# Stage orders rewritten in a two-layer hybrid DeltaNet, attention and Mamba-2 step, and six stored slots per DeltaNet tile in place of seven

## The reference

```python
h    = rms_norm(x, norm_w) * (1 + scale) + shift        # shift, scale, gate = silu(cond) @ w_mod + b_mod
proj = h @ w_in                                          # 1024 -> 8800 columns, split over the mixers
a    = gated_rms(gdn(forward) + rev(gdn(backward)))      # DeltaNet, 4 heads of 128, chunks, two directions
b    = softmax_attention(rope(norm(q)), rope(norm(k)), v) * silu(z_b)          # 8 heads, 2 KV heads, 64
c    = rms_norm((ssd(forward) + rev(ssd(backward)) + D * x) * silu(z_c), ssm_norm_w)  # 16 heads of 64
merged = sig(g_a) * (a @ w_branch_a) + sig(g_b) * (b @ w_branch_b) + sig(g_c) * (c @ w_branch_c)
x = x + gate * (merged @ w_out)
```

## Time and profile before

| | before |
|---|---|
| median of 3 runs | 4101.25 us (4098.83 to 4103.64) |
| profiled execution | 4097.26 us, span 4095.5 us |
| PE busy | 3728.9 us, 91% of the span |
| DVE / ACT / POOL busy | 52% / 26% / 19% |
| chain that ended last | PE 60%, issue 10%, DVE 9%, DMA 8% |
| DMA | 521 MB, mean 127 GB/s |

### The profile page before, as it was taken

How to read it: one execution, slowest core, us unless ns; L and a number is a source line. 1 busy time by engine, 2 the same in 40 slices (tenths; PEclk the granted TensorE clock), 3 DMA queues, 4 the chain that set the end, 5 groups by cost and what they waited for, 6 DMA issues and landing times.

```text
span 4095.5 us, 71558 instructions
## 1 busy us (share of the span) xinstructions
PE 3728.9 (91%) x29139; PEld 3486.7 (85%) x29139; DVE 2123.8 (52%) x2421; ACT 1049.0 (26%) x1910; POOL 762.4 (19%) x778
## 2 busy tenths in 40 slices
PE   6999999999799788889989999999987987888898
PEld 3999999999688565889989999999986875578898
DVE  3631353233577676586465125523336876846853
ACT  3211120112345461311122102111224546232210
POOL 1110111132400243131011101112232013511400
PEclk8999999999899899999989999999999998999999
DMA  7332232233611467644233322323335117675532
GB/s 221 105 103 87 78 95 90 72 120 107 257 44 37 148 233 240 231 139 106 93 109 116 100 76 82 93 79 99 118 134 192 38 43 235 230 244 186 118 104 86
DMA packets 375283, 521.13 MB, mean 127 GB/s; under 512 B 83089, under 2 KB 293833, under 8 KB 372017
## 3 DMA queue, kind: packets, MB, share of 16 engines
q1 hardware_dynamic: 327992, 393.58, 29.2%
q0 software_dynamic: 36256, 104.28, 9.4%
q10 hardware_dynamic: 10720, 18.88, 1.4%
HBM read 340.20 MB, written 176.45 MB: 126 GB/s over the span
## 4 chain that ended last, share of the span: by engine, by line
PE 60%; issue 10%; DVE 9%; DMA 8%; DVEq 4%; SPq 4%; ACT 2%; POOL 2%; POOLq 0%; ACTq 0%
PE PSUM L807 10%; PE PSUM L808 10%; PE PSUM L809 10%; PE PSUM L1368 3%; DMA proj_d<-leave 3%; PE PSUM L1521 2%; PE PSUM L1355 2%; PE PSUM L1283 2%; PE PSUM L1285 2%; PE PSUM L1284 2%; PE PSUM L1653 2%; PE PSUM L1654 2%; PE PSUM L1655 2%; PE PSUM L1334 1%; DMA qk_t<-proj_d 1%
## 5 line engine op out<-in xcount | busy, mean ns | idle before, releaser
L807 PE MATMUL PSUM<-h_hi,w_hi 128*128 128x384 f32 x2400 | 806.4, 336 | 8.2 <-DVEq L2495 8.2
L808 PE MATMUL PSUM<-h_lo,w_hi 128*128 128x384 f32 x2400 | 804.3, 335 | 0.0
L809 PE MATMUL PSUM<-h_hi,w_lo 128*128 128x384 f32 x2400 | 804.2, 335 | 0.0
L807 PEld LDWEIGHTS PSUM<-h_hi,w_hi 128*128 128x128 f32 x2400 | 452.6, 189 | 12.7 <-DVEq L2495 8.9
L808 PEld LDWEIGHTS PSUM<-h_lo,w_hi 128*128 128x128 f32 x2400 | 452.6, 189 | 0.0
L809 PEld LDWEIGHTS PSUM<-h_hi,w_lo 128*128 128x128 f32 x2400 | 452.5, 189 | 0.0
L2169 POOL DMA_DIRECT2D proj_d<-leave x140 | 142.5, 1018 | 1450.8 <-DVE leave L2491 567.2
L1283 PE MATMUL PSUM<-h_hi,w_hi 128*128 128x384 f32 x960 | 328.0, 342 | 4.0 <-ACT ssm_rows L1806 4.0
L1284 PE MATMUL PSUM<-h_lo,w_hi 128*128 128x384 f32 x960 | 323.8, 337 | 0.0
L1285 PE MATMUL PSUM<-h_hi,w_lo 128*128 128x384 f32 x960 | 323.6, 337 | 0.0
L2599 DVE TENSOR_REDUCE row_max<-PSUM 128x1 f32<-128x1152 f32 x128 | 173.5, 1355 | 98.3 <-PE PSUM L1335 98.2
(11 more groups left out here) (387 smaller groups left out, 7393.7 us busy)
## 6 DMA issues: line engine op xcount, KB each, us to landing
proj_d<-leave POOLq DMA_DIRECT2D x140, 512.0 KB, 3.9
w_raw<-in_w_in SPq DMA_DIRECT2D x54, 1024.0 KB, 5.1
gdn_tile_d<-g_out SPq DMA_DIRECT2D x18, 1792.0 KB, 7.3
wide_br<-proj_d SPq DMA_DIRECT2D x48, 576.0 KB, 4.4
xs<-ssm_tok_d SPq DMA_DIRECT2D x32, 640.0 KB, 5.6
ssm_tok_d<-x_rest SPq DMA_DIRECT2D x36, 512.0 KB, 3.1
w_in<-in_w_in SPq DMA_DIRECT2D x16, 1024.0 KB, 6.2
w_next<-in_w_mod SPq DMA_DIRECT2D x16, 1024.0 KB, 8.4
```

What stands on the lines that cost most here:

```text
L807: pe.matmul(dst, wh, x_hi[:, k, lo:hi], start=(k == 0), stop=False)
L808: pe.matmul(dst, wh, x_lo[:, k, lo:hi], start=False, stop=False)
L809: last = pe.matmul(dst, wl, x_hi[:, k, lo:hi], start=False, stop=(k == kt - 1))
```

## The change

- Tail: DVE does `rotate` and `low_parts` before `split_tail`. SP issues the first `ain` loads before the stores of `ssm_rows`; PE waits for `ssm_rows` before the first turn of heads, and no longer ahead of the tail.
- Start: the load of `w_mod[3]` waits until six token tiles are turned, and shares a semaphore with a token load, so that one becomes free (`w_high`).
- DeltaNet preparation: 6 slots per tile. DVE multiplies bank 4 by each direction's decay (slots 0 and 5), adds the two decays in place, and multiplies bank 3 by the sum once (slot 2: one direction's triangle below the diagonal, the other's above, their sum on it). The scaled keys lie in slots 1 and 4, the values in 3. `solve_begin` halves the diagonal. The scan's loads take slots 2:4 as one piece, and the low or high triangle is read from the same slot.
- SSM preparation: the loads of tile 0's decay rows are issued in the attention stage; the modulation product runs at tiles 1 to 8 in place of 0 to 7, its copy is one of 128x256 in place of four of 2x256, DVE zeroes that bank once in place of two POOL clears.
- SSM scan: the loads of DeltaNet tile 1 are issued by ACT, right behind those of tile 0, in place of SP after the last step; SP arrives at barrier 5 right behind its last scan load and stores the final states afterwards. The first tile of the scan waits for all of them.
- Branches: new places in `BESIDE` (four `y` jobs beside branch b, five beside a); the weight of the SSM norm is multiplied into `w_branch_c` as this is split, so `weigh_y` is gone; the low part `low_y_b` is made by DVE; the high copies of full-depth weights are made by ACT (`weights_high`, semaphore `w_high`), and DVE's `split_in_place` waits for them; `y_sq` is laid out so that ACT writes with a stride of 8 elements and DVE reads it in sequence; all nine `low_o` come before the last `merge_first`.

```diff
--- before.py
+++ after.py
@@ -82,17 +82,12 @@
-BESIDE = ({1: ("y", 0), 3: ("o", 0), 5: ("o", 1), 7: ("y", 1), 9: ("o", 2), 11: ("o", 3), 13: ("o", 4),
-           15: ("o", 5), 17: ("o", 6), 19: ("o", 7), 21: ("o", 8), 23: ("y", 2)},
-          {1: ("y", 3), 4: ("y", 4), 7: ("y", 5), 10: ("y", 6), 13: ("y", 7), 16: ("y", 8)},
+BESIDE = ({1: ("y", 0), 3: ("o", 0), 5: ("o", 1), 6: ("y", 1), 8: ("o", 2), 10: ("o", 3), 12: ("o", 4),
+           13: ("y", 2), 15: ("o", 5), 17: ("o", 6), 19: ("o", 7), 21: ("o", 8), 22: ("y", 3)},
+          {5: ("y", 4), 8: ("y", 5), 11: ("y", 6), 14: ("y", 7), 17: ("y", 8)},
           {})
...
@@ -315,7 +310,7 @@
-        y_sq = place(a, "y_sq", [P, KT, P])
+        y_sq = place(a, "y_sq", [P, P, KT])
...
@@ -671,45 +666,41 @@
-            return (l * (33 - 2 * p) + count) * 16
+            return (l * (33 - 8 * p) + count) * 16
...
@@ -671,45 +666,41 @@
         def tile_loads(e, t):
             for d in range(2):
                 tt = tile_of(t, d)
-                in_ = scan_in[d][t % 2] if t else beta_in
-                e.dma_start(av_t[d][t % 2][:], gdn_tile_d[tt, :, 3 * d:3 * d + 4:3]).then_inc(in_, 16)
+                in_ = scan_in[d][t % 2] if t > 1 else beta_in
+                e.dma_start(av_t[d][t % 2][:], gdn_tile_d[tt, :, 2:4]).then_inc(in_, 16)
                 e.dma_start(qk_t[d][t % 2][:], proj_d[tt, :, B_GDN:B_GDN + 8]).then_inc(in_, 16)
         def kq_loads(e, t):
             for d in range(2):
-                e.dma_start(kq_t[d][t % 2][:], gdn_tile_d[tile_of(t, d), :, 3 * d + 1:3 * d + 3]).then_inc(kq_in[t % 2], 16)
+                e.dma_start(kq_t[d][t % 2][:], gdn_tile_d[tile_of(t, d), :, 4 * d:4 * d + 2]).then_inc(kq_in[t % 2], 16)
...
@@ -776,12 +767,33 @@
         def split_in_place(dve, l, g):
-            n, p = G_ATT + g, g % 2
+            p, last = g % 2, None
             hi, (raw, lo) = (half_hi[p], half_lo[p]) if g < 8 else (full_hi[p], full_lo[p])
-            dve.wait_ge(w_loaded[p], 16 * split_count(l, n // 2) + 16)
-            dve.tensor_copy(hi[:], raw[:])
-            dve.drain()
-            dve.tensor_tensor(lo[:], raw[:], hi[:].bitcast(F32), ALU.subtract).then_inc(w_ready[p], 1)
+            if g < 8:
+                dve.wait_ge(w_loaded[p], 16 * split_count(l, (G_ATT + g) // 2) + 16)
+                dve.tensor_copy(hi[:], raw[:])
+                dve.drain()
+            else:
+                dve.wait_ge(w_high, l * 8 + g - 7)
+            if 8 <= g < 12:
+                for k in range(KT):
+                    last = dve.scalar_tensor_tensor(lo[:, k], raw[:, k], vec[:, V_SNORM + k:V_SNORM + k + 1], hi[:, k].bitcast(F32), ALU.mult, ALU.subtract)
+            else:
+                last = dve.tensor_tensor(lo[:], raw[:], hi[:].bitcast(F32), ALU.subtract)
+            last.then_inc(w_ready[p], 1)
+        def weights_high(act, l, g):
+            n, p, last = G_ATT + g, g % 2, None
+            hi, raw = full_hi[p], full_lo[p][0]
+            act.wait_ge(w_loaded[p], 16 * split_count(l, n // 2) + 16)
+            if 8 <= g < 12:
+                for k in range(KT):
+                    last = act.activation(hi[:, k], raw[:, k], ACT.Copy, scale=vec[:, V_SNORM + k:V_SNORM + k + 1])
+            else:
+                last = act.activation(hi[:], raw[:], ACT.Copy)
+            last.then_inc(w_high, 1)
...
@@ -893,6 +897,16 @@
                 ain_load(0)
                 ain_load(1)
+                sp.wait_ge(row_made, l * 3 + 3)
+                flat_rows = ssmrow_d.rearrange("t d r n -> (t d r) n")
+                sp.dma_start(flat_rows[0:512].rearrange("(c p) n -> p c n", p=P), ssm_rows[:, 0:4].bitcast(F32)).then_inc(row_out, 16)
+                sp.dma_start(flat_rows[512:576], ssm_rows[0:64, 4].bitcast(F32)).then_inc(row_out, 16)
+                sp.wait_ge(row_out, l * 80 + 80)
+                sp.sem_inc(waits_held, 1)
...
@@ -1002,16 +1016,11 @@
-                    sp.wait_ge(ssm_prod[d], l * 17 + 16)
-                    sp.sem_inc(waits_held, 1)
-                tile_loads(sp, 1)
-                inverse_loads(sp, 1)
-                kq_loads(sp, 1)
+                barrier(sp, l, 5)
...
@@ -1268,8 +1279,6 @@
-                pe.wait_ge(row_made, l * 3 + 3)
-                pe.sem_inc(waits_held, 1)
                 for i in range(N_TAIL):
...
@@ -1457,25 +1466,27 @@
-                    if t < NS:
-                        pe.wait_ge(mod_in[t % 2], l * 64 + (t // 2) * 16 + 32)
+                    if t:
+                        pe.wait_ge(mod_in[(t - 1) % 2], l * 64 + ((t - 1) // 2) * 16 + 32)
                         pe.wait_ge(sp_cb, n + 1)
-                        mod_parts(7, w_next[t % 2], GW)
+                        mod_parts(7, w_next[(t - 1) % 2], GW)
...
@@ -1980,6 +1988,9 @@
                 inverse_loads(act, 0)
+                tile_loads(act, 1)
+                kq_loads(act, 1)
+                inverse_loads(act, 1)
...
@@ -2034,42 +2045,43 @@
-                    act.activation(y_sq[:], y_t[:, t], ACT.Square).then_inc(squared, 1)
+                    act.activation(y_sq[:].rearrange("p t k -> p k t"), y_t[:, t], ACT.Square).then_inc(squared, 1)
...
@@ -2034,42 +2045,43 @@
-                for s, (what, t) in BESIDE[0].items():
-                    if s == 23:
-                        act.wait_ge(acc_ready[1], acc_done(l, G_ATT + 3, 1))
-                        for q in range(3):
-                            o_high(q)
+                for what, t in BESIDE[0].values():
                     if what == "y":
                         square_y(t)
                     elif t + 1 < NT:
                         square_o(t + 1)
-                for t in range(3, NT):
+                act.wait_ge(acc_ready[1], acc_done(l, G_ATT + 3, 1))
+                for t in range(NT):
                     o_high(t)
-                act.wait_ge(lo_made, nth(l, NT - 1, 0, 2) + 1)
-                high = 0
-                for _, t in BESIDE[1].values():
-                    while high < t - 1:
-                        y_high_b(high)
-                        high += 1
-                    square_y(t)
-                for t in range(high, NT):
+                act.wait_ge(lo_made, nth(l, NT - 1, 0, 3) + 1)
+                for t in range(4):
                     y_high_b(t)
+                for s in range(24):
+                    if s == 21:
+                        act.wait_ge(y_summed, l * NT + NT)
+                        act.sem_inc(waits_held, 1)
+                    if s == 21:
+                        weights_high(act, l, 8)
+                    if s in BESIDE[1]:
+                        t = BESIDE[1][s][1]
+                        square_y(t)
+                        y_high_b(t)
                 act.wait_ge(acc_ready[1], acc_done(l, G_GDN + 3, 1))
                 for t in range(NT):
                     y_high_a(t)
+                weights_high(act, l, 9)
...
@@ -2243,6 +2259,11 @@
+                def decay_rows(t, d):
+                    pool.dma_start(s_row[d][32:34].rearrange("s h n -> s (h n)"), ssmrow_d[t, d].rearrange("(s h) n -> s (h n)", s=2)).then_inc(s_in[d], 16)
+                    pool.dma_start(s_col[d][0:32], ssmrow_d[t, d]).then_inc(s_in[d], 16)
+                for d in range(2):
+                    decay_rows(0, d)
...
@@ -2310,21 +2327,8 @@
-                def weigh_y(t):
-                    pool.wait_ge(squared, squared_at(l, "y", t))
-                    pool.tensor_tensor(y_t[:, t], y_t[:, t], over(vec[:, V_SNORM:V_SNORM + 8], P), ALU.mult).then_inc(pool_made, 1)
-                def low_y_b(t):
-                    pool.wait_ge(hi_made, nth(l, t, 1, 3) + 1)
-                    pool.tensor_tensor(y_lo[:, t, 4:KT], y_t[:, t, 4:KT], y_hi_b[:, :, cols(t)].bitcast(F32), ALU.subtract).then_inc(pool_made, 1)
-                o_power(0)
-                for what, t in BESIDE[0].values():
-                    if what == "y":
-                        weigh_y(t)
-                    elif t + 1 < NT:
-                        o_power(t + 1)
-                for step, t in Y_STEPS[3:]:
-                    (weigh_y if step == "w" else low_y_b)(t)
+                for t in range(NT):
+                    o_power(t)
...
@@ -2553,12 +2557,13 @@
-                    if i and TAIL + i + 1 < G_ATT:
-                        split_tail(TAIL + i + 1)
                     if i < NT:
                         rotate(i)
                         dve.drain()
                     low_parts(i)
+                    if i and TAIL + i + 1 < G_ATT:
+                        split_tail(TAIL + i + 1)
...
@@ -2581,15 +2586,16 @@
-                        last = dve.tensor_tensor(by_head(g_out[p][:, 2 + 2 * d]), by_head(bank(1)), over(e_rest[:, d, t, 0:4], GD), ALU.mult)
+                        last = dve.tensor_tensor(by_head(g_out[p][:, 1 + 3 * d]), by_head(bank(1)), over(e_rest[:, d, t, 0:4], GD), ALU.mult)
                     last.then_inc(scaled, 1)
                     dve.wait_ge(gp_e, n + 1)
                     dve.wait_ge(gp_k, n + 1)
```

(26 more changed lines are left out.)

108 lines of the change are left out of this document (51 added, 57 removed).

## The result

The changed kernel takes 4024.02 us (median of 4 runs, 4022.17 to 4033.07), the one before 4100.04 us (4 runs, 4093.22 to 4103.64): ratio 0.9821, 95% interval 0.9801 to 0.9841. A second series gave 4032.99 against 4105.72, ratio 0.9824 (0.9802 to 0.9845). The gain is 73 to 76 us by the medians, where 69.4 was forecast.

What follows compares the result with a forecast made beforehand. PE was taken to set the time in most of the span. Five terms, largely one layer doubled, summed to -69.4 us from 4097.3: 4027.9 in the profiled execution, 4032 as median; 8 in 10 lie in 4000 to 4070.

Steps and rivals of the forecast that it cites:

- Tail, -24.8 forecast: Tail, both layers: 21.4 us of PE's waits go and 3.4 of lower clock returns; bounds -28.3 to -12.
- I take half: Tail: the lower clock after PE's waits costs 6.9 us together, of which 3.4 was counted as regained.
- Rival 4: Tail: POOL, not the casts, ends each chain, so the tail gives only 8 us: 4049; chance 0.06.
- DeltaNet preparation, -1.4 forecast: DeltaNet preparation: same DVE time within 0.1, a smaller store waited for less; between -3 and +1 us.
- SSM preparation, -9 forecast: SSM preparation: PE's waits for `s_col` and `w_next` go but don't add up, POOL's later loads hold; -4.5 us per layer.
- Scan and barrier, -8.2 forecast: SSM scan and barrier 5: SP arrives at once, -5.1 us per layer, less contention; bounds -12 and +4 for two layers.
- the +1 taken: SSM scan: tile 1's loads share full DMA engines, so the steps stretch, +1 us per layer.
- The second rival: SSM scan: moved loads halve SP's stream, steps go from 7.2 to 7.6 us, the 8 us are lost: 4040; chance 0.08.
- Branches, -26 forecast: Branches: less DVE load without POOL beside it shortens branch a, branch b pays +3.5; -13 us per layer, bounds -8 to -36.
- the first unit of c, 15.5 becomes 13.7: Start of branch c: the wait for POOL's last low parts goes, -1.8 us per layer.
- Rival 1: Branch a: DVE bounds it whatever POOL does, so the branches give nothing: 4058; chance 0.09.
- Rival 3: Branches: DVE waits at `w_high`, delaying merges and PE's banks; 6.5 us lost per group gives 4109; chance 0.04.

## Why the prediction was right, term by term

The time, 4032 for 4024 to 4033, and the sum, -69.4 for -73 to -76, were right. Their closeness is in part luck: of the terms, two compensate, the tail with 7 us more than forecast and the branches with 9.5 less.

- **Tail, -24.8 forecast, -32 measured**, by the stages outside its own bound of -28.3 (by the times alone, 27 to 42, the bound would still do). Waits and chain were as forecast: all seven waits for `q_hl` gone, both at the start as well, `w_lo` never late. The step that failed is "I take half" of the clock. All of it came back, because no wait was left in the tail for the clock to fall after: the matmuls of its three lines, 975.4 us in all on the page of before, take 967.5, so the clock was worth 7.9. With the 21.4 us of waits that is 29.3. Another 1.6 is in the turns behind the waits, L1259, of which 72 take 9.0 us in a layer in place of 9.8; what is left, under 2 us, no row assigns. Rival 4 is refuted: all seven waits went, not a third of them.
- **DeltaNet preparation, -1.4 forecast**, -1.0 by the stages (2 x -0.5), and open between 0 and 18 by the times, as said. That the stage keeps its length was right.
- **SSM preparation, -9 forecast, -8.8 by the stages and -10.5 alone.** Right in size and mechanism: the waits did not add up, and it is POOL's loads behind the stored inverse that took over. The run with the rows early shows it: moving just these gives another 5.7 per layer.
- **Scan and barrier, -8.2 forecast, -7.7 by the stages, -5.1 alone.** The barrier's 6.7 became 1.6, as worked out (-5.1). Contention is larger than the +1 taken: the SSM scan as a whole gained only 2.0, so it pays some 3 per layer, of which the longer waits for `c_t` are 2.3 in layer 0; the page of the profile has `xs` landing after 7.3 us in place of 5.6. The DeltaNet scan, counted at nothing, is 1.8 shorter (its waits for `qk_t` went from 8.1 to 5.8 in layer 0), but no run shows that this part did it. Without that 1.8 the term by the stages is -4.0, half of the forecast. The second rival, SP's row held down to half of the stream, would have given the 8 us back: the gain of 4 to 8 in all ways of counting speaks against it, though part of its mechanism, the steps made longer by the shared stream, is there.
- **Branches, -26 forecast, -16.5 by the stages**, the term that was mis-sized: -13 per layer was taken, -8.3 came, and the miss is on both sides of the start of branch c. Branches b and a together were to give -16.2 + 3.5 = -12.7; over all layers they gave 4.2 - 13.8 = -9.6. What branch a becomes was right: 59.9 for 59.3, L2828 (now L2841) at 1.36, no POOL, DVE 49.8 of 59. What it comes from was not: 75.5 was read in one layer, where ten layers have 73.6 on average and at most 75.2. In that one layer the change looks like the forecast (140.6 became 128.6, -12.1).
  The second step that failed is "the first unit of c, 15.5 becomes 13.7". From its first matmul, that unit took 14.5 and 16.1 in the kernel before and takes 17.0 and 17.2 in the changed one, and branch c as a whole went from 103.0 to 104.3 on average. The gain was to come from "POOL's last low parts", but POOL had finished them at 1851.6, and what PE waited for until 1858.0 was DVE's `full_lo`, 1.4 us. After the change PE waits 1.7 there for the last `y_lo`, which DVE makes behind the eight parts of `full_lo` (3.25 us from 1815.87), and then does 5.6 us at the lower of its two levels (0.79 over 16 us). One thing that was covered at nothing lies ahead of it: ACT's write of `y_sq` over a stride takes 2.20 and not 1.06, and the last sum on DVE waited 1.7 for it. But it is not what the wait at branch c hangs on alone, since with the squares in the old order the wait is 2.6: DVE's last two sums then take 1.5 longer, against 1.1 less of waiting for ACT.
- **Rival 1**, POOL innocent of the long additions, is refuted by POOL's work put back: the addition is at 2.03 again, and branch a at 72.5 where it was 73.6 before. The branches as a whole are then above those of before (246 for 241.4), because branch b keeps the jobs that were moved beside it. Rival 3 did not come up: no wait for `w_high` by DVE reached PE.

## What to carry to other kernels

Where two operations run on one engine between a wait's release and the next engine's need, put what is needed first and the large split behind it; here that was worth more than all else, and the clock came back with the waits. An elementwise step on POOL that nobody waits for is still paid for by DVE's copies and additions of two SBUF inputs beside it (39 us of POOL beside branch a cost DVE 15.6 us and made the branch 12.7 longer), so folding it into a weight split can gain time. When two waits in a row are removed, look for the third (here a DMA issue parked behind a store it does not need) before adding them up, and look for the last operation of a stage, since PE can lose more by the clock behind a wait of under 2 us than by the wait. And read a stage's length in both layers, and in more than one profile if there are any, before taking a difference from it.
